# Other byte distances between the moving operands and the weights of a two-block network on one core

## The reference

```python
h = rmsnorm(x, norm_mix[i])
p = h @ w_in[i]
...
x = x + jnp.concatenate([y_a, y_b, y_c], axis=-1) @ w_out[i]
h = rmsnorm(x, norm_ffn[i])
up = dwconv3(h @ ffn_w_up[i], ffn_conv_w[i], ffn_conv_b[i])
gate, val = jnp.split(up, 2, axis=-1)
x = x + (jax.nn.silu(gate) * val) @ ffn_w_down[i]
...
proj = h @ w_in
...
merged = (jax.nn.sigmoid(ga) * (ya @ w_up_a)
          + jax.nn.sigmoid(gb) * (yb @ w_up_b)
          + jax.nn.sigmoid(gc) * (yc @ w_up_c))
return x + merged @ w_o
```

## Time and profile before

| | |
|---|---|
| median of 3 executions | 2485.74 us (2481.35 to 2487.22) |
| profiled execution | 2486.66 us, its span 2485.0 us |
| mean granted TensorE clock | 0.986 |
| TensorE busy | 2413.7 us (97%) in 19,960 matmuls |
| weight loads busy | 2373.9 us (96%) |
| VectorE, ScalarE busy | 1536.2 us (62%), 1136.0 us (46%) |
| DMA | 400.43 MB, mean 161 GB/s |

### The profile page before, as it was taken

How to read it: one execution, slowest core, us unless ns; L and a number is a source line. 1 busy time by engine, 2 the same in 40 slices (tenths; PEclk the granted TensorE clock), 3 DMA queues, 4 the chain that set the end, 5 groups by cost and what they waited for, 6 DMA issues and landing times.

```text
span 2485.0 us, 50887 instructions
## 1 busy us (share of the span) xinstructions
PE 2413.7 (97%) x19960; PEld 2373.9 (96%) x19960; DVE 1536.2 (62%) x2064; ACT 1136.0 (46%) x1463; POOL 12.8 (1%) x27
## 2 busy tenths in 40 slices
PE   6999999999999999996899999999999999999999
PEld 6898999999999999996899999999999999999999
DVE  6556577667546667567876666776576554544554
ACT  5343345555434555434444445544465443434443
POOL 0000000000000000000000000000000000000000
PEclk9999899999999999998999999999999999999999
DMA  6353365555555555553333333333355365555554
GB/s 233 134 187 118 125 189 186 186 187 188 191 187 187 186 187 189 189 188 122 114 120 117 108 112 122 113 121 118 137 164 165 115 204 177 188 178 176 187 189 160
DMA packets 110149, 400.43 MB, mean 161 GB/s; under 512 B 12394, under 2 KB 12421, under 8 KB 109904
## 3 DMA queue, kind: packets, MB, share of 16 engines
q1 hardware_dynamic: 108000, 391.00, 47.8%
q0 software_dynamic: 2032, 7.67, 0.9%
HBM read 396.52 MB, written 2.10 MB: 160 GB/s over the span
## 4 chain that ended last, share of the span: by engine, by line
PE 92%; DVE 5%; ACT 1%; issue 1%; DMA 0%; DVEq 0%; SPq 0%; ACTq 0%
PE bank L418 91%; ACT w_hi L918 1%; DVE w_lo L1345 1%; DVE scratch L1394 1%; PE bank L620 1%; DVE s_k L1394 0%; DMA x<-in_xT 0%; DVE h_lo L1391 0%; DVE cum L1391 0%; DVE ping L1391 0%; DVE s_t L1391 0%; DVE root L1433 0%; DVE acc L1391 0%; DVE s_t L1398 0%; DVE s_k L1391 0%
## 5 line engine op out<-in xcount | busy, mean ns | idle before, releaser
L1345 DVE TENSOR_TENSOR w_lo<-raw,w_hi 128x1024 fp32r<-128x1024 f32 x736 | 896.9, 1224 | 794.6 <-ACT w_hi L918 789.8
L918 ACT ACTIVATE w_hi<-raw 128x1024 fp32r<-128x1024 f32 x736 | 778.9, 1060 | 1092.1 <-PE bank L418 1070.2
L418 PE MATMUL bank<-h_hi,w_hi 128*128 128x256 f32 x4016 | 1150.4, 286 | 26.9 <-DVE w_lo L1345 8.4
L418 PE MATMUL bank<-h_lo,w_hi 128*128 128x256 f32 x4016 | 1127.2, 281 | 0.0
L418 PE MATMUL bank<-h_hi,w_lo 128*128 128x256 f32 x4016 | 1126.0, 280 | 0.0
L418 PEld LDWEIGHTS bank<-h_hi,w_hi 128*128 128x128 f32 x4016 | 761.7, 190 | 36.4 <-issue 14.5
L418 PEld LDWEIGHTS bank<-h_lo,w_hi 128*128 128x128 f32 x4016 | 762.0, 190 | 3.3 <-issue 2.2
L418 PEld LDWEIGHTS bank<-h_hi,w_lo 128*128 128x128 f32 x4016 | 761.1, 190 | 0.0
L418 PE MATMUL bank<-m_hi,w_hi 128*128 128x256 f32 x704 | 196.5, 279 | 0.0
L418 PE MATMUL bank<-m_lo,w_hi 128*128 128x256 f32 x704 | 196.5, 279 | 0.0
L418 PE MATMUL bank<-m_hi,w_lo 128*128 128x256 f32 x704 | 196.5, 279 | 0.0
(11 more groups left out here) (413 smaller groups left out, 2777.5 us busy)
## 6 DMA issues: line engine op xcount, KB each, us to landing
raw<-in_units SPq DMA_DIRECT2D x736, 512.0 KB, 4.2
x<-in_xT SPq DMA_DIRECT2D x4, 512.0 KB, 5.9
memx<-in_memT POOLq DMA_DIRECT2D x4, 512.0 KB, 7.7
out_y<-obuf SPq DMA_DIRECT2D x8, 256.0 KB, 4.3
bias_t<-in_bias POOLq DMA_DIRECT2D x8, 192.0 KB, 2.9
dft<-in_dft POOLq DMA_DIRECT2D x1, 1024.0 KB, 7.8
decay<-in_decay POOLq DMA_DIRECT2D x1, 768.0 KB, 5.9
con<-in_con SPq DMA_DIRECT2D x1, 546.0 KB, 8.0
```

The lines of the kernel that those rows point to most:

```text
L418: return pe.matmul(out, lhsT, rhs, start=start, stop=stop, skip_group_check=True)
L918: return act.activation(out, in_, ACT.Copy, scale=scale)
L1345: dve.tensor_tensor(w_lo[slot][:, :, :], raw[slot][:, :, :], w_hi[slot][:, :, :].bitcast(F32), ALU.subtract).then_inc(split_done, 1)
```

## The change

The tiles of five moving operands are put at other places modulo 128 bytes. `h_hi` and `h_lo` become views of one tile `h`, 4 floats behind its start. `shifted` makes a tile with room for `skip` floats ahead and returns a view behind them. With the offsets given, hi and lo of an operand have the same distance from the weights. Since `h` is 32 bytes larger than the two tiles were, the arena begins at 64 modulo 128 instead of 32.

| operand | distance before | distance now |
|---|---|---|
| `h` | 32 | 48 |
| `y` | 32 | 72 |
| `m` | 32 | 80 |
| `ya` | 32 | 40 |
| `mg` | 32 | 56 |
| `mh` (not in the diff) | 32 | 64 |

```diff
-        h_hi = sb("h_hi", [P, KT, T], F32R)
-        h_lo = sb("h_lo", [P, KT, T], F32R)
+        h_both = sb("h", [P, 2 * KT * T + 8], F32R)
+        h_hi, h_lo = (h_both[:, 4 + i * KT * T:4 + (i + 1) * KT * T].rearrange("p (k t) -> p k t", t=T)
+                      for i in range(2))
...
+        def shifted(name, tiles, at, skip):
+            flat = place(name, [P, (skip + 7) // 8 * 8 + tiles * T], at, F32R)
+            return flat[:, skip:skip + tiles * T].rearrange("p (k t) -> p k t", t=T)
+
         K = 1024
-        spare = place("spare", [P, 8], 105 * K)
-
-        y_hi = place("y_hi", [P, KT, T], 0, F32R)
-        y_lo = place("y_lo", [P, KT, T], 16 * K, F32R)
+        spare = place("spare", [P, 8], 106752)
+
+        y_hi = shifted("y_hi", KT, 0, 2)
+        y_lo = shifted("y_lo", KT, 16 * K + 32, 26)
...
-        m_hi = place("m_hi", [P, FF_HALF, T], 0, F32R)
-        m_lo = place("m_lo", [P, FF_HALF, T], 22 * K, F32R)
+        m_hi = shifted("m_hi", FF_HALF, 0, 4)
+        m_lo = shifted("m_lo", FF_HALF, 22 * K + 32, 28)
...
-        ya_hi = place("ya_hi", [P, 24, T], 24 * K, F32R)
-        ya_lo = place("ya_lo", [P, 24, T], 48 * K, F32R)
-        gate = place("gate", [P, 2, T], 72 * K)
-        macc = place("macc", [P, 2, T], 74 * K)
-        mtmp = place("mtmp", [P, 2, T], 76 * K)
-
-        mg_hi = place("mg_hi", [P, KT, T], 78 * K, F32R)
-        mg_lo = place("mg_lo", [P, KT, T], 0, F32R)
+        ya_hi = shifted("ya_hi", 24, 24 * K, 26)
+        ya_lo = shifted("ya_lo", 24, 48 * K + 128, 26)
+        gate = place("gate", [P, 2, T], 72 * K + 256)
+        macc = place("macc", [P, 2, T], 74 * K + 256)
+        mtmp = place("mtmp", [P, 2, T], 76 * K + 256)
+
+        mg_hi = shifted("mg_hi", KT, 78 * K + 256, 30)
+        mg_lo = shifted("mg_lo", KT, 0, 30)
```

## The result

The changed kernel takes 2507.86 us (median of 4 executions, 2505.66 to 2509.28); the kernel before, on the same chip, 2486.1 (4 executions, 2481.35 to 2487.22). The ratio is 1.0091 with a 95% interval of [1.0077, 1.0105]: **slower by 0.9%**, where 2441 was forecast.

A forecast was written before the change was run, and what follows sets the result against it. TensorE was taken as the bound, busy 2413.7 of 2485.0 us. Gains of `h` 23.5, `m` 12.4, `y` 3.7, `mh` 3.0, `mg` 2.2 and `ya` 1.1 sum to 45.9: 2486.7 - 45.9 = 2441 us, range 2395 to 2532.

The forecast's parts named there:

- 7.8 ns over the transposes' pace: Wide matmuls: 116.8 ns each against 109 for the fp32 transposes; 137 us in all, what the change can play for.
- The rival that no distance matters: Wide matmuls keep their pace at any distance, as the Trainium skill's rule has it: 2486.7 us, chance 0.27.
- The count of matmuls a tile: Wide matmuls: `h` 12,048, `m` 2112, `ya` 1152, `y`, `mh` and `mg` 768 each; 17,616 in all.
- the cost of nothing for the writers and the transposes: Writers of moving tiles: idle time covers any slowdown; transposes could lose 0.7 us, left out.
- none at 96, and a straight line between: Wide matmuls: excess of 7.8 ns at distance 32, none at 96, 0.122 ns a byte between; gain 45.9 us.
- Distance modulo 128: Moving tiles: their distances from the weights counted modulo 128 bytes, 32 for all five named tiles before the change.
- One bound of a rival: Large-gain rival: the new distances leave the overlap, pace 109 to 112 ns, 2349 to 2395 us; chance 0.08.
- `h` pays a fourth: Slower rival: leaving 32 adds a fourth hold-up of 2.6 ns per `h` matmul, 31 us, 2518; all tiles 2532; chance 0.29.
- deciding point: `h` stretches: the slower rival decides from the point where their pace passes 117.1 ns.
- its sign in the grouped view: Profile after, means by tile: `h` reading 281 to 282 ns would show the fourth hold-up.
- nothing says that 32 is the better part: Argument against the slower rival: 32 came about by the sizes of the tables ahead of `h`.
- a count of meetings: Wide matmuls: the matmul's and the load's readers meet, and 7.8 ns is close to three hold-ups of 2.7.

The follow-up runs named there:

- e12_still: Kernel before, with the up projection's moving operand one column read 256 times and the down projection's weights one column read 128 times: 2464.89 us against 2487.26.
- e7_w16_h32: Kernel before, with weights and `h` 16 bytes further modulo 256 (`h` distance 32) and the arena 48 behind the weights: 2507.73 us, ratio 1.0086.
- f3_w16_all16: Kernel before, with weights 16 bytes further and moving tiles at their old places modulo 256, so every distance is 16: 2513.79 us, ratio 1.0107.
- f1_h16_rest32: Kernel before, with `h` moved to distance 16 and the arena kept at 32 modulo 256: 2489.01 us, ratio 1.0008.
- f2_h16_rest64: Kernel before, with `h` moved to distance 16 and the arena to 64 modulo 256: 2491.11 us, ratio 1.001.
- e11_h16_rest128: Kernel before, with `h` moved to distance 16 and the arena to 128 modulo 256: 2502.58 us, ratio 1.0057.
- f4_h24_rest32: Kernel before, with `h` moved to distance 24 and the arena kept at 32 modulo 256: 2520.43 us, ratio 1.0134.
- e6_all288: Kernel before, with `h` and the arena 256 bytes further, every moving tile at distance 288: 2487.23 us, ratio 1.0006.
- e5_all160: Kernel before, with `h` and the arena 128 bytes further, every moving tile at distance 160: 2503.99 us, ratio 1.0073.

## Why the prediction was wrong

**What held.** TensorE's pace is the bound, and each ns of it reaches the span: the two engines behind the earlier trace rows changed nothing but their idle time. Of the 7.8 ns over the transposes' pace 5.0 go when the moving operand stands still (`e12_still`), and the places of the two operands set the pace, 116.7 to 120.1 ns on average over a tile's matmuls, with 113.3 in some stretches. The rival that no distance matters is refuted. The count of matmuls a tile was right, and so was the cost of nothing for the writers and the transposes.

**What failed** is one step: "none at 96, and a straight line between". It took the end of the line from fp32 matmuls of 128 columns, another form. For the wide form 96 is, with 0, the worst place that was measured (120.1 ns instead of the 109 that the line ends in), 48 costs 1.5 ns more than 32 instead of 1.95 less, and 24 costs 3.3 more. No wide matmul of any run reached 109 with both operands walking. With the sign of each term wrong, 45.9 us of gain became some 22 of loss. I had 0.122 ns a byte from two points of another form, and the price of every tile hung on it; the text called it "not a measured curve" and forecast by it all the same.

**The modulus** was wrong too. "Distance modulo 128" was taken from the change; the period is 256, so that `y_lo`, `m_lo`, `ya_hi` and both tiles of `mg` lay at distances that the sum didn't know. The 109 ns of the transposes belong to 224 modulo 256 and not to 96, and no run has a wide matmul at 224. So the runs don't tell whether the wide form differs from the small one at the same place; they tell that it costs 120 ns where the line had none of the surplus. One bound of a rival was also off: a pace of 112 would be (116.8 - 112) x 17,616 = 85 us, 2402 and not 2395.

**The rival that came true**, in its sign, is the slower one: "`h` pays a fourth" when it leaves the part with the smaller count. Its deciding point, 117.1 ns in the `h` stretches, was passed (118.3), and its sign in the grouped view, 281 to 282 for `h`, is what the profile after shows. Its price was too high by 1.1 ns a matmul for `h`, 2.6 forecast and 1.5 measured, and for `m` (1.1), too low for `mg` (3.3) and `ya` (3.6). Against it stood "nothing says that 32 is the better part". Nothing said the opposite either; of all the places measured, none gives a faster kernel than 32. That the forecast had a chance for it, 0.29, and a range that takes in 2507.86 is no merit of the mechanism that it was made with. Whether the mechanism is a count of meetings is not shown: the runs give paces, and they take a few values again and again (113.3, 116.7, 117.8, 118.7, 120.0), which would fit a whole number of hold-ups spread over several matmuls, but no row shows a single one.

**What stays open.** The rule by which the two places together give a pace (`e7_w16_h32` has 118.3 ns at distance 32 and 116.7 at 48, `f3_w16_all16` 117.3 to 120.0 at 16, where `f1_h16_rest32` has 117.0); whether the surplus is paid where two readers meet; what chooses the rhythm with which a stretch begins, and so whether the 113.3 ns could be had throughout. Were it held in all 17,616 wide matmuls, 3.4 ns each would be 60 us, an estimate. No kernel of the table holds it throughout; `mg` in `f2_h16_rest64` and the second up projection in `e11_h16_rest128` come closest.

## What to carry to other kernels

Where TensorE runs back to back with a weight load for every matmul, the places of weights and moving operand modulo 256 bytes are worth up to 2% here between the best and the worst that were measured: measure a few, each for all tiles at once, before reasoning about one. Don't take the curve from another type or width of matmul. Compare the pace from start to start in stretches without waits, which tells 1 ns apart, where the time of the kernel needs many executions for it; and look at several stretches, since the same places can give 113.3 ns in one and 118.7 in the next.

## What the runs showed of the hardware

- A wide fp32r matmul with its own weight load takes 113.3 to 120.1 ns at full clock with both operands walking (`mg` in `f2_h16_rest64`, `h` in `f4_h24_rest32`), and 111.7 with a moving operand read from one place (`e12_still`). With weights read from one place it took 113.3 in one stretch and 116.6 in another.
- A shift of the moving tiles by 256 bytes leaves the time (`e6_all288`, 1.0006 [0.9996, 1.0015]), a shift by 128 doesn't (`e5_all160`, 1.0073 [1.0056, 1.0089]). The weights' place counts too: 16 bytes further take `m` from 116.7 to 120.0 ns (`f3_w16_all16`), and leave `h` at 118.3 at another place (`e7_w16_h32`).
- The same places can have several steady rhythms, which last for hundreds of us: `h` at 118.7 ns in the first up projection of `e11_h16_rest128` and at 113.3 in the second. Places equal modulo 256 took 734.74 and 741.73 us for the same 6292 matmuls (`e6_all288`). Part of the spread of 0.2 to 0.5% between executions of a kernel may be that; no kernel has two traces that would show it.
- 8 bytes more of distance (`h` at 16 and at 24, the rest at 32) cost 3.1 ns a matmul, 2.6%: 117.0 and 120.1 ns.
